# Column sums of the second half's last four squares on TensorE, and input chunks ahead of the last additions to x, in both feed-forward parts

## The chip, the cores and the metric

The kernel runs on one core of one Trainium2 chip. A core has TensorE (PE, matrix products), VectorE (DVE), ScalarE (ACT), GpSimd (POOL), and SyncE (SP), whose queue issues the transfers here. Each takes its instructions in program order and waits on semaphores. The metric is the device time of one execution in microseconds (us); lower is better. The kernel before takes 2377.08 us, the median of three runs (2376.66 to 2378.32).

## The reference

A backbone block of two layers over 1024 tokens of 1024 features, in float32. Layer 0 mixes tokens by latent attention, layer 1 by a short gated convolution; each is followed by a feed-forward part. What matters here is how each part normalises x and adds its result back:

```python
def rmsnorm(x, w):
    xf = x.astype(jnp.float32)
    y = xf * lax.rsqrt(jnp.mean(xf * xf, axis=-1, keepdims=True) + NORM_EPS)
    return (y * w.astype(jnp.float32)).astype(x.dtype)

def modulate(h, shift, scale):
    return h * (1 + scale) + shift
...
        x = x + g1 * y
        x = x + g2 * swiglu(modulate(rmsnorm(x, norm_ffn[i]), sh2, sc2),
                            ffn_w_gate[i], ffn_w_up[i], ffn_w_down[i])
```

## The kernel before

The program is written by hand for each engine, so its order on an engine is the order of the text. x is kept transposed: eight tiles of 128 features (m or k = 0 to 7), each with two halves of 512 tokens, A and B. Every product is made of three matmuls of 128x512 on a high and a low part of each operand (`mm3`, L607 to L609), named `_hi` and `_lo`.

An addition to x is `to_x(d, m, gate)` on DVE (L2071): bank m of the product d times the gate, plus x. A half's root mean square is a "job": ACT squares the eight x tiles (`squares_of`, L1393), POOL adds them one after another into one tile `acc` (`squares_sum`, L2766), PE sums that tile over its partitions against a column of ones (`job_sum`, L853: four products of 128x1, one for each 128 tokens), ACT takes the root (`job_sqrt`, L1400), DVE the reciprocal on a diagonal (`job_diag`), PE spreads it over all partitions (`job_bcast`, L871), and ACT copies that to `rstd` (`job_out`, L1405). Then the input chunks h of that half are made: for each k DVE scales x by `rstd` (`h_scaled`, L2285), ACT adds the shift and rounds to `h_hi` (L1628), and DVE makes `h_lo` (L2292). In `h_chunks`, DVE issues the scaling of chunk k+1 before the low part of k, since there are two buffers `tmp`.

A feed-forward part (`ffn_wino`; the first is f0, the second f1) begins with one block of four units in the plain form: unit 0 and 1 work on half A, unit 2 and 3 on half B (`inner`), each 8 chunks of 6 matmuls, into PSUM banks 0 and 1 or 2 and 3. After it come ten blocks in a Strassen-like form (`wino_block`), whose operands on the input's side (named T1 to T4) are sums of parts of h of both halves. The half-A statistic is ready ahead of unit 0. That of half B (jobs `J_MIX+1` and `J_MIX+5`, called job B here) is made in unit 0 and 1: its squares run between the A chunks, its column sum stands after chunk 5 of unit 0 and its broadcast after chunk 0 of unit 1. From the broadcast ACT and DVE then make the eight B chunks (`h_full_of`, `h_full_chunks`), multiply unit 1 (`silu_of`, `ffn_inner`), form T3, T1 and T2, and ACT rounds T2 (`b_top`) before it takes the SiLU of unit 3. The second product of the first Strassen-like block (GATE, "A12") writes to the bank that unit 3 used, so PE waits there for the SiLU of unit 3 (`bank_read`).

Ahead of each part stand the last additions of the half B of x: tiles 0 to 3 are added first, tiles 4 to 7 then take turns with the A chunks 0 to 3.

The buffers `raw` and `rq` share memory: `rq` (weights of the Strassen-like blocks) is loaded by SP once both `raw` tiles have been used.

## Time and profile before

| | |
|---|---|
| median of three runs | 2377.08 us (2376.66 to 2378.32) |
| profiled execution, its time | 2377.69 us |
| span of its trace | 2375.9 us |
| PE busy | 2334.4 us (98%) |
| DVE busy | 1690.1 us (71%) |
| ACT busy | 806.6 us (34%) |
| POOL busy | 151.2 us (6%) |
| mean granted TensorE clock | 0.992 of full speed |

Times in the rows below are microseconds from the start of the span. In a timeline row the first number is the start, the second the duration (of all instructions of a merged row), then the engine, line and operation; in brackets stands how long the engine had been idle and who released it. A matmul's duration overlaps that of the next, so the pace of PE is read from the distance of the starts. A float32 column product is recorded as two entries (x8 is four products). Unit 0 of f0 begins at 655.88 us, that of f1 at 1682.11 us.

### The profile page before, as it was taken

To read this page: it belongs to the slowest core of one execution; us is meant where nothing else is said; L and a number is where in the kernel's file an instruction comes from. 1 tells how busy PE (TensorE), PEld (TensorE's weight loads), DVE (VectorE), ACT (ScalarE), POOL (GpSimd) and SP (SyncE) were. 2 spreads that over 40 slices of the span, in tenths; PEclk is the share of its full clock that TensorE was granted. 3 is DMA by queue.
4 is the path that set the end of the run, shared out by engine and by line. 5 is a ranking of instruction groups with operands and counts; after the bars stand their busy time and mean duration, and the time that the engine had idled before them with its cause. 6 is when DMAs were issued, how large, how long until landed. Compare 5 with 4: busy or idle time off the path is not lost.

```text
span 2375.9 us, 29068 instructions
## 1 busy us (share of the span) xinstructions
PE 2334.4 (98%) x10989; PEld 1928.3 (81%) x10989; DVE 1690.1 (71%) x2495; ACT 806.6 (34%) x1279; POOL 151.2 (6%) x109
## 2 busy tenths in 40 slices
PE   7989999999999999999999999999999999999998
PEld 4878888887878888888888788888788888888887
DVE  4667777786589788888887763364897777777766
ACT  6345545454343222222222511111522222222224
POOL 0111111200210000000001200000200000000002
PEclk9999999999999999999999999999999999999998
DMA  7101111122201333333322020120101111111111
GB/s 290 38 25 43 42 42 51 42 80 107 80 36 62 107 107 107 107 107 107 107 98 89 18 71 27 45 72 27 45 28 53 54 54 54 54 52 51 52 50 71
DMA packets 48055, 163.33 MB, mean 69 GB/s; under 512 B 5185, under 2 KB 6593, under 8 KB 47809
## 3 DMA queue, kind: packets, MB, share of 16 engines
q1 hardware_dynamic: 47936, 161.72, 19.8%
q8 instruction: 78, 1.28, 0.2%
q14 instruction: 41, 0.33, 0.0%
HBM read 157.51 MB, written 4.19 MB: 68 GB/s over the span
## 4 chain that ended last, share of the span: by engine, by line
PE 94%; DVE 3%; ACT 1%; DMA 1%; POOL 0%; issue 0%; SPq 0%; ACTq 0%; DVEq 0%; POOLq 0%
PE ps L607 26%; PE ps L609 26%; PE ps L608 26%; PE ps L1062 3%; PE ps L996 2%; PE ps L1000 2%; PE ps L998 2%; PE ps L997 2%; PE ps L1001 1%; PE ps L1041 1%; PE ps L1043 1%; PE ps L1042 1%; DVE h_lo L2292 1%; DMA ada_ring<-ada_pe 1%; PE ps L1084 1%; PE ps L853 1%
## 5 line engine op out<-in xcount | busy, mean ns | idle before, releaser
L2071 DVE SCALAR_TENSOR_TENSOR x<-ps,mods,x 128x512 f32<-128x512 f32 x448 | 328.9, 748 | 151.4 <-PE ps L609 131.9
L607 PE MATMUL ps<-g_hi,w_hi 128*128 128x512 f32 x832 | 324.9, 390 | 0.8 <-DVE x L2071 0.6
L608 PE MATMUL ps<-g_lo,w_hi 128*128 128x512 f32 x832 | 323.8, 389 | 0.0
L609 PE MATMUL ps<-g_hi,w_lo 128*128 128x512 f32 x832 | 323.7, 389 | 0.0
L607 PE MATMUL ps<-h_hi,op_hi 128*128 128x512 f32 x640 | 249.2, 389 | 0.0
L609 PE MATMUL ps<-h_hi,op_lo 128*128 128x512 f32 x640 | 249.0, 389 | 0.0
L1657 ACT CAST op_hi<-rq 128x512 fp32r<-128x512 f32 x240 | 147.3, 623 | 235.6 <-PE ps L609 231.4
L1668 ACT ACTIVATE g_full<-g_full 128x512 f32<-128x512 f32 x80 | 50.8, 635 | 495.3 <-DVE g_full L2412 495.2
L607 PE MATMUL ps<-h_hi,w_hi 128*128 128x512 f32 x512 | 200.9, 392 | 7.5 <-DVE h_lo L2292 7.5
L609 PE MATMUL ps<-h_hi,w_lo 128*128 128x512 f32 x512 | 199.3, 389 | 0.0
L608 PE MATMUL ps<-h_lo,w_hi 128*128 128x512 f32 x512 | 199.3, 389 | 0.0
L608 PE MATMUL ps<-h_lo,op_hi 128*128 128x512 f32 x480 | 186.7, 389 | 0.0
L608 PE MATMUL ps<-w_lo,op_hi 128*128 128x512 f32 x480 | 186.7, 389 | 0.0
L607 PEld LDWEIGHTS ps<-g_hi,w_hi 128*128 128x128 f32 x832 | 156.2, 188 | 35.4 <-DVE x L2071 2.5
L609 PEld LDWEIGHTS ps<-g_hi,w_lo 128*128 128x128 f32 x832 | 156.2, 188 | 32.6
L608 PEld LDWEIGHTS ps<-g_lo,w_hi 128*128 128x128 f32 x832 | 156.2, 188 | 32.1
L1925 DVE TENSOR_TENSOR op_lo<-rq,op_hi 128x512 fp32r<-128x512 f32 x240 | 163.0, 687 | 1.1
L1925 DVE TENSOR_TENSOR pt_lo<-ps,pt_hi 128x512 fp32r<-128x512 f32 x160 | 110.1, 688 | 72.1 <-ACT pt_hi L1481 71.6
L609 PEld LDWEIGHTS ps<-h_hi,op_lo 128*128 128x128 f32 x640 | 120.1, 188 | 25.0
L607 PEld LDWEIGHTS ps<-h_hi,op_hi 128*128 128x128 f32 x640 | 120.2, 188 | 24.9
L1481 ACT CAST pt_hi<-ps 128x512 fp32r<-128x512 f32 x160 | 93.9, 587 | 131.3 <-PE ps L1062 131.3
L607 PE MATMUL ps<-w_hi,op_hi 128*128 128x512 f32 x320 | 124.5, 389 | 0.0
(345 smaller groups left out, 4569.7 us busy)
## 6 DMA issues: line engine op xcount, KB each, us to landing
rq<-stream SPq DMA_DIRECT2D x80, 512.0 KB, 3.5
mod_raw_f<-ada_rows SPq DMA_DIRECT2D x48, 512.0 KB, 3.6
raw<-stream SPq DMA_DIRECT2D x46, 512.0 KB, 3.6
w_lo_f<-stream SPq DMA_DIRECT2D x46, 512.0 KB, 4.4
mod_raw<-ada_rows SPq DMA_DIRECT2D x32, 512.0 KB, 3.5
ada_ring<-ada_pe SPq DMA_DIRECT2D x16, 512.0 KB, 10.9
x<-x_t SPq DMA_DIRECT2D x8, 512.0 KB, 7.3
out_t<-x SPq DMA_DIRECT2D x16, 256.0 KB, 2.1
```

The lines of the kernel that those rows point to most:

```text
L607: nc.tensor.matmul(out, w[0][wi], a[0][ai], start=start, stop=False)
L608: nc.tensor.matmul(out, w[0][wi], a[1][ai], start=False, stop=False)
L609: return nc.tensor.matmul(out, w[1][wi], a[0][ai], start=False, stop=stop)
L996: nc.tensor.matmul(dst, qa[par][0][:, q], ckv_hi[:, k0:k1], start=True, stop=False)
L997: nc.tensor.matmul(dst, qa[par][1][:, q], ckv_hi[:, k0:k1], start=False, stop=False)
L998: nc.tensor.matmul(dst, qa[par][0][:, q], ckv_lo[:, k0:k1], start=False, stop=False)
L1062: last = nc.tensor.transpose(ps[:, bank, j * P:(j + 1) * P], pbuf[:, 4 * (gb % 2) + j, k * P:(k + 1) * P], ident[:])
L1481: copy(pt_hi[:, (10 * gb + k) % 4, :], ps[:, bank, :]).then_inc(ra, 1)
L1657: copy(op_hi[:, at % 4, :], operand_a(s, mat, name)).then_inc(op_h, 1)
L1668: nc.scalar.activation(gate, gate, ACT.Silu).then_inc(corner_act, 1)
L1925: return nc.vector.tensor_tensor(dst, full, hi.bitcast(F32), ALU.subtract)
L2071: nc.vector.scalar_tensor_tensor(out=x[:, m, HALF[half]], in0=ps[:, out_bank(d, m), :], scalar=mods[:, gate + m:gate + m + 1], in1=x[:, m, ...
```

## The change

In both feed-forward parts:

- ACT squares tiles 0 to 3 of half B ahead of all A chunks, and POOL adds only these (three additions instead of seven).
- DVE makes all eight A chunks, and only then adds tiles 4 to 7 to x.
- ACT squares those four tiles into a buffer of their own, `sq_tail`, in memory that `rq` uses later. `job_sum` then sums five tiles (`acc` and the four of `sq_tail`) on PE: 20 column products instead of 4. SP's first `rq` loads now wait for this sum (`st_sum`) instead of for the product before.
- PE makes the sum after chunk 2 of unit 1 instead of chunk 5 of unit 0, and the broadcast after chunk 5 instead of chunk 0 of unit 1.
- ACT takes the SiLU of unit 0 before the root instead of after it, and rounds the second `down` tile behind the root. On DVE the products of unit 0 stand ahead of the diagonal.

```diff
--- before.py
+++ after.py
@@ -472,6 +472,7 @@
     mod_raw_f = sb("mod_raw_f", [D], F32, G1)
     sq_a = [sb(f"sq_a{k}", [HT], F32, X0 + 8192 + 2048 * k) for k in range(2)]
     acc_a = sb("acc_a", [HT], F32, N0)
+    sq_tail = sb("sq_tail", [4, HT], F32, X0)
     bsb = [sb(f"bsb{f}", [HT], F32, X0 + 2048 * f) for f in range(2)]
     zb = [sb(f"zb{f}", [T + 2], F32, X0 + 4096 + 4128 * f) for f in range(2)]
     op_hi, op_lo = sb("op_hi", [4, HT], F32R, N0), sb("op_lo", [4, HT], F32R, N0 + 8192)
@@ -559,6 +560,8 @@
     sq_end, fin_a, fin_p = sem("sq_end"), sem("fin_a"), sem("fin_p")
 
     sq_last = [tmp[0], tmp[1], ab[0], ab[1]]
+    tail_set = sem("tail_set")
+    TAIL_JOBS = (J_MIX + 1, J_MIX + 5)
 
     HALF = (slice(0, HT), slice(HT, T))
     ALL = slice(None)
@@ -797,7 +800,7 @@
                 modf_in(n)
 
         stream_in(12, 14)
-        sp.wait_ge(dn, 8 * D_F0)
+        sp.wait_ge(st_sum, J_MIX + 2)
         sp.wait_ge(t_lo, 14)
         quads_first(0)
         for s in range(WINO):
@@ -810,6 +813,7 @@
                     .then_inc(in_cv[n], 16)
         sp.wait_ge(op_l, product_n(WINO - 1, GATE, "S4") + 1)
         stream_in(14, len(TILES))
+        sp.wait_ge(st_sum, J_MIX + 6)
         sp.wait_ge(t_lo, len(TILES))
         quads_first(WINO)
         for s in range(WINO, 2 * WINO):
@@ -833,10 +837,13 @@
 
             bank = job_banks(j)[0]
             parts = (acc_of(j), sq[0]) if job_n(j) == QL else (acc_of(j),)
+            if j in TAIL_JOBS:
+                parts = (acc_of(j), *(sq_tail[:, n, :] for n in range(4)))
+                pe.wait_ge(tail_set, 4 * (TAIL_JOBS.index(j) + 1))
             if j <= J_XB:
                 pe.wait_ge(sq_row, j + 1)
             elif job_n(j) == D:
-                C.add("sqa", KD - 1)
+                C.add("sqa", 3 if j in TAIL_JOBS else KD - 1)
                 pe.wait_ge(sqa, C.at("sqa"))
             elif job_n(j) == QL:
                 C.add("q_sq", 2)
@@ -1302,8 +1309,8 @@
 
         def ffn_wino(phase, turn, job_b, job_a):
 
-            inner(phase, 0, 0, turn, (job_b, 5), None)
-            inner(phase, 0, 1, turn, None, (job_b, 0))
+            inner(phase, 0, 0, turn, None, None)
+            inner(phase, 0, 1, turn, (job_b, 2), (job_b, 5))
             inner(phase, 0, 2, turn, None, None)
             inner(phase, 0, 3, turn, None, None)
             for s in range(WINO):
@@ -1621,6 +1628,12 @@
             act.wait_ge(xe, 8 * d + m + 1)
             squares(j, m, x[:, m, HALF[j % 2]], HT)
 
+        def squares_tail(j, d):
+
+            for n in range(4):
+                act.wait_ge(xe, 8 * d + n + 5)
+                nc.scalar.activation(sq_tail[:, n, :], x[:, n + 4, HALF[j % 2]], ACT.Square).then_inc(tail_set, 1)
+
         def h_top_of(turn, half, k):
 
             shift, _ = AFTER[turn]
@@ -1753,10 +1766,11 @@
         def ffn_wino(phase, turn, d_before, jobs_b, jobs_a):
 
             s0 = 0 if phase == "f0" else WINO
-            for f in range(2):
-                top(phase, 0, "down", f, (dn, 8 * d_before + 8))
+            squares_tail(jobs_b, d_before)
+            top(phase, 0, "down", 0, (dn, 8 * d_before + 8))
+            silu_of(phase, 0, 0)
             job_sqrt(jobs_b)
-            silu_of(phase, 0, 0)
+            top(phase, 0, "down", 1, (dn, 8 * d_before + 8))
             job_out(jobs_b)
             for k in range(KD):
                 h_full_of(turn, k)
@@ -1868,12 +1882,10 @@
                 gate_out(blk, "b", B, 1)
                 job_sqrt(jobs_a)
                 job_out(jobs_a)
-                for m in range(3):
+                for m in range(4):
                     squares_of(jobs_a + 1, d + 1, m)
                 for k in range(KD):
                     h_top_of(turn + 1, A, k)
-                    if k < 5:
-                        squares_of(jobs_a + 1, d + 1, k + 3)
 
         for n in range(4, 6):
             top("out", 0, "wo", n)
@@ -1897,12 +1909,10 @@
         job_sqrt(J_MIX)
         job_out(J_MIX)
         act.wait_ge(sv_set, 1)
-        for m in range(3):
+        for m in range(4):
             squares_of(J_MIX + 1, D_OUT + 3, m)
         for k in range(KD):
             h_top_of(0, A, k)
-            if k < 5:
-                squares_of(J_MIX + 1, D_OUT + 3, k + 3)
         ffn_wino("f0", 0, D_OUT + 3, J_MIX + 1, J_MIX + 2)
         conv_start(1, J_MIX + 3)
         conv(1, J_MIX + 3, J_MIX + 4)
@@ -2555,10 +2565,10 @@
         def ffn_wino(phase, turn, gate, job_b, job_a):
 
             s0 = 0 if phase == "f0" else WINO
-            for f in range(2):
-                low(phase, 0, "down", f)
+            ffn_inner(phase, 0, 0)
+            low(phase, 0, "down", 0)
             job_diag(job_b)
-            ffn_inner(phase, 0, 0)
+            low(phase, 0, "down", 1)
             h_full_chunks(turn)
             ffn_inner(phase, 0, 1)
             operand_low(s0, 0)
@@ -2707,10 +2717,9 @@
                 job_diag(job_a)
                 to_x(d_b, 2, gate)
                 to_x(d_b, 3, gate)
-                for k in range(4):
-                    h_chunks(turn + 1, A, k, k + 1)
-                    to_x(d_b, k + 4, gate)
-                h_chunks(turn + 1, A, 4, KD)
+                h_chunks(turn + 1, A, 0, KD)
+                for m in range(4, KD):
+                    to_x(d_b, m, gate)
 
         rest = slice(N_PE_MOD + N_ATT_MOD - 8, N_PE_MOD + N_ATT_MOD)
         dve.wait_ge(mod_out, passes + 1)
@@ -2744,10 +2753,9 @@
         to_x(D_OUT + 3, 2, GATES[0])
         to_x(D_OUT + 3, 3, GATES[0])
         dve.wait_ge(sv_set, 1)
-        for k in range(4):
-            h_chunks(0, A, k, k + 1)
-            to_x(D_OUT + 3, k + 4, GATES[0])
-        h_chunks(0, A, 4, KD)
+        h_chunks(0, A, 0, KD)
+        for m in range(4, KD):
+            to_x(D_OUT + 3, m, GATES[0])
         ffn_wino("f0", 0, GATES[1], J_MIX + 1, J_MIX + 2)
         conv_start(1, GATES[1])
         conv(1, GATES[2], J_MIX + 3, J_MIX + 4)
@@ -2806,12 +2814,10 @@
 
         def squares_sum(j):
 
-            for m in range(1, KD):
+            for m in range(1, 4 if j in TAIL_JOBS else KD):
                 add_squares(j, m, HT)
 
-        squares_sum(J_MIX)
-        squares_sum(J_MIX + 1)
-        for j in range(J_MIX + 2, J_MIX + 7):
+        for j in range(J_MIX, J_MIX + 7):
             squares_sum(j)
         for m in range(1, KD // 2):
             add_squares(J_MIX + 7, m, HT)
```

In the rows of the program's order below, PE stands in unit 0 of f0 before, at the column sum of job B (`acc_104` is its accumulated tile):

```order
L608 MATMUL ps<-h_lo,w_hi 128x512
L609 MATMUL ps<-h_hi,w_lo 128x512
L853 MATMUL ps<-ones,acc_104 128x1 x4
L607 MATMUL ps<-h_hi,w_hi 128x512
L608 MATMUL ps<-h_lo,w_hi 128x512
L609 MATMUL ps<-h_hi,w_lo 128x512
```

And in unit 1 of f0 now, between chunk 2 and chunk 3 (each `x4` row is the four `sq_tail` tiles):

```order
L612 MATMUL ps<-h_hi,w_lo 128x512
L860 MATMUL ps<-ones,acc_104 128x1
L860 MATMUL ps<-ones,sq_tail 128x1 x4
L860 MATMUL ps<-ones,acc_104 128x1
L860 MATMUL ps<-ones,sq_tail 128x1 x4
L860 MATMUL ps<-ones,acc_104 128x1
L860 MATMUL ps<-ones,sq_tail 128x1 x4
L860 MATMUL ps<-ones,acc_104 128x1
L860 MATMUL ps<-ones,sq_tail 128x1 x4
L610 MATMUL ps<-h_hi,w_hi 128x512
```

The sum has moved from unit 0 to unit 1 and has grown from 4 column products to 20.

DVE at the start of f0 before, from the first A chunk (`tmp` is the scaled x, L2071 an addition to x):

```order
L2292 SCALAR_TENSOR_TENSOR h_lo<-tmp_107,mods,h_hi 128x512
L2071 SCALAR_TENSOR_TENSOR x<-ps,mods,x 128x512
L2285 SCALAR_TENSOR_TENSOR tmp_107<-x,svec,rstd_105 128x512
L2292 SCALAR_TENSOR_TENSOR h_lo<-tmp_108,mods,h_hi 128x512
L2071 SCALAR_TENSOR_TENSOR x<-ps,mods,x 128x512
L2285 SCALAR_TENSOR_TENSOR tmp_108<-x,svec,rstd_105 128x512
L2292 SCALAR_TENSOR_TENSOR h_lo<-tmp_107,mods,h_hi 128x512
L2071 SCALAR_TENSOR_TENSOR x<-ps,mods,x 128x512
```

DVE there now, from the last A chunks to job B's reciprocal:

```order
L2295 SCALAR_TENSOR_TENSOR tmp_108<-x,svec,rstd_105 128x512
L2302 SCALAR_TENSOR_TENSOR h_lo<-tmp_107,mods,h_hi 128x512
L2302 SCALAR_TENSOR_TENSOR h_lo<-tmp_108,mods,h_hi 128x512
L2081 SCALAR_TENSOR_TENSOR x<-ps,mods,x 128x512 x4
L2322 TENSOR_TENSOR ab_153<-ab_153,ps 128x512
L2325 CAST g_hi<-ab_153 128x512
L1935 TENSOR_TENSOR g_lo<-ab_153,g_hi 128x512
L1935 TENSOR_TENSOR w_lo<-raw_109,w_hi 128x1024
L1941 RECIPROCAL rr<-sd 128x4
L1944 TENSOR_TENSOR diag<-ident,rr 128x512
L1935 TENSOR_TENSOR w_lo<-raw_110,w_hi 128x1024
```

The additions stood between the chunks and now stand behind the last one; the multiplication of unit 0 (`ab`) and one low part of a `down` tile have moved ahead of the reciprocal.

ACT around job B's root in f0 before (`sd` is the root, `ab` the SiLU):

```order
L1628 ACTIVATE h_hi<-tmp_108,mods 128x512 [waits s_h_mul]
L1413 CAST w_hi<-raw_109 128x1024 [waits s_dn,s_in_raw0]
L1413 CAST w_hi<-raw_110 128x1024 [waits s_dn,s_in_raw1]
L1400 ACTIVATE sd<-ps,eps_c 128x4 [waits s_st_dg,s_st_sum]
L1636 ACT_TABLE_LOAD
L1636 ACTIVATE ab_153<-ps 128x512 [waits s_pj]
L1405 COPY rstd_106<-ps 128x512 [waits s_st_bc]
L1642 ACTIVATE w_hi_f<-tmp_107,mods 128x512 [waits s_h_mul]
```

ACT there now:

```order
L1635 ACTIVATE sq_tail<-x 128x512 [waits s_xe] x4
L1420 CAST w_hi<-raw_109 128x1024 [waits s_dn,s_in_raw0]
L1649 ACT_TABLE_LOAD
L1649 ACTIVATE ab_153<-ps 128x512 [waits s_pj]
L1407 ACT_TABLE_LOAD [waits s_st_dg]
L1407 ACTIVATE sd<-ps,eps_c 128x4 [waits s_st_sum]
L1420 CAST w_hi<-raw_110 128x1024 [waits s_dn,s_in_raw1]
L1412 COPY rstd_106<-ps 128x512 [waits s_st_bc]
L1655 ACTIVATE w_hi_f<-tmp_107,mods 128x512 [waits s_h_mul]
```

And ACT now at the SiLU of unit 1, behind the last B chunk:

```order
L1655 ACTIVATE w_lo_f<-tmp_108,mods 128x512 [waits s_h_mul]
L1658 CAST h_hi<-w_lo_f 128x512 [waits s_b_set]
L1649 ACT_TABLE_LOAD
L1649 ACTIVATE ab_154<-ps 128x512 [waits s_pj]
L1670 CAST op_hi<-rq 128x512 [waits s_in_q0,s_n_lo]
L1670 CAST op_hi<-rq 128x512 [waits s_in_q0]
```

The order SiLU, root, SiLU takes three loads of ACT's function table where one stood: one ahead of the first SiLU, one ahead of the root and one ahead of the SiLU of unit 1, which had none of its own.

## Rows read from the trace of the kernel before

**Rows 1.** The page: busy time by engine, and the chain that ended last

```profile
PE 2334.4 (98%) x10989; PEld 1928.3 (81%) x10989; DVE 1690.1 (71%) x2495; ACT 806.6 (34%) x1279; POOL 151.2 (6%) x109
...
PE 94%; DVE 3%; ACT 1%; DMA 1%; POOL 0%; issue 0%; SPq 0%; ACTq 0%; DVEq 0%; POOLq 0%
```

**Rows 2.** Waits of PE, whole run: who waited, for whom, us, times, longest

```profile
PE ps L607 <- DVE h_lo L2292: 7.5, 6, 1.7
```

**Rows 3.** Timeline, PE, f0: start of unit 0, and the broadcast of job B

```profile
655.88 0.39 PE L607 MATMUL ps<-h_hi,w_hi 128*128 128x512 f32 x1
...
671.89 1.05 PE L871 MATMUL ps<-diag,ones 128*128 128x128 f32 x8
```

**Rows 4.** Timeline, PE, f1: unit 0, the sum and the broadcast of job B

```profile
1682.11 0.43 PE L607 MATMUL ps<-h_hi,w_hi 128*128 128x512 f32 x1
...
1697.03 0.95 PE L853 MATMUL ps<-ones,acc 128*128 128x1 f32 x8
1697.83 0.47 PE L607 MATMUL ps<-h_hi,w_hi 128*128 128x512 f32 x1
...
1702.04 1.05 PE L871 MATMUL ps<-diag,ones 128*128 128x128 f32 x8
```

**Rows 5.** Timeline, DVE, f1: an A chunk while POOL adds, and two without it

```profile
1692.29 1.75 DVE L2292 SCALAR_TENSOR_TENSOR h_lo<-tmp,mods,h_hi 128x512 fp32r<-128x512 f32 x1
1694.07 0.75 DVE L2285 SCALAR_TENSOR_TENSOR tmp<-x,svec,rstd 128x512 f32<-128x512 f32 x1
...
1695.52 0.75 DVE L2285 SCALAR_TENSOR_TENSOR tmp<-x,svec,rstd 128x512 f32<-128x512 f32 x1
```

**Rows 6.** Timeline, ACT, f1: first h_hi, the table load, SiLU of units 0 and 1

```profile
1682.01 0.71 ACT L1628 ACTIVATE h_hi<-tmp,mods 128x512 fp32r<-128x512 f32 x1
...
1699.10 1.28 ACT L1636 ACT_TABLE_LOAD   x1
1700.39 0.60 ACT L1636 ACTIVATE ab<-ps 128x512 f32<-128x512 f32 x1
...
1716.01 0.60 ACT L1636 ACTIVATE ab<-ps 128x512 f32<-128x512 f32 x1
```

**Rows 7.** Timeline, PE, a sum of eight column products (16 entries), and what follows

```profile
72.99 0.28 PE L853 MATMUL ps<-ones,acc 128*128 128x1 f32 x2
...
74.69 0.47 PE L607 MATMUL ps<-x0a_hi,sw_hi 128*128 128x512 f32 x1
```

**Rows 8.** Timeline, DVE, ACT, PE, f1: unit 1 multiplied, to the second product (1736.97)

```profile
1716.74 0.68 DVE L2312 TENSOR_TENSOR ab<-ab,ps 128x512 f32<-128x512 f32 x1
...
1734.15 1.92 ACT L1662 CAST w_hi<-w_lo_f 128x2048 fp32r<-128x2048 f32 x1 [9.64 <-DVE w_lo_f L2377]
1735.97 0.59 ACT L1636 ACTIVATE ab<-ps 128x512 f32<-128x512 f32 x1
...
1736.29 0.39 PE L607 MATMUL ps<-h_hi,op_hi 128*128 128x512 f32 x1
...
1736.97 0.39 PE L607 MATMUL ps<-h_hi,op_hi 128*128 128x512 f32 x1
```

**Rows 9.** The same in f0: SiLU of unit 3, and the second product

```profile
705.83 0.59 ACT L1636 ACTIVATE ab<-ps 128x512 f32<-128x512 f32 x1
...
706.82 0.39 PE L607 MATMUL ps<-h_hi,op_hi 128*128 128x512 f32 x1
```

**Rows 10.** Timeline, PE: two restarts after a wait, and the end of the first slow stretch

```profile
29.65 0.76 PE L607 MATMUL ps<-x0a_hi,sw_hi 128*128 128x512 f32 x1 [2.58 <-DVE sw_lo L1964]
...
34.05 0.47 PE L608 MATMUL ps<-x0a_lo,sw_hi 128*128 128x512 f32 x1
...
123.13 0.58 PE L996 MATMUL ps<-ckv_hi,qa_hi 128*128 128x256 f32 x1 [3.25 <-ACT pbuf L1518]
```

**Rows 11.** Windows, closing column sum (from 2356.3): PE, PEld, DVE, ACT, POOL busy, then PEclk

```profile
2357.00:2358.00 1.00, 1.00 (x12) 1.00 (x11) 1.00 (x3) 0.63 (x1) 0.00 (x0) 1.00 0.62 240
...
2359.00:2360.00 1.00, 1.00 (x7) 1.00 (x6) 1.00 (x3) 0.98 (x2) 0.00 (x0) 0.50 0.39 150
```


## The prediction

> **What bounds the kernel now.** I read the page first: PE is busy for 98% of the span, and 94% of the chain that ended last is PE's [rows 1]. So only time in which PE stands still, or work put on PE, can move the end. The list of PE's waits comes next. Its largest entry that belongs to the feed-forward parts is the wait for `h_lo`: 7.5 us in 6 waits [rows 2], all in unit 0 of f0 and f1. The timeline gives the true size of what can be won. Three wide matmuls take 1736.97 - 1736.29 = 0.68 us [rows 8], so one is 0.227 us, a chunk of six 1.36 us and a unit of eight chunks 10.88 us. In f1, unit 0 starts at 1682.11 and its chunk 6 at 1697.83 [rows 4]; less six chunks (8.16) and the sum (0.80) that is 6.8 us of standing still. In f0 the broadcast starts at 671.89, 16.01 us after unit 0 [rows 3]; nine chunks (12.24) and the sum take 13.0 of it, so some 2.9 us are lost, 9.7 us together. The last thing I read is what follows the broadcast of job B, since the change makes it later: the rows from unit 1 on to the second product of the first Strassen-like block [rows 8, 9].
>
> **Part 1: A chunks ahead of the additions.** An A chunk takes DVE 1695.52 - 1694.07 = 1.45 us where nothing interferes, and the low part alone 1.75 us while POOL adds [rows 5]. PE uses one each 1.36 us. With the four additions behind the chunks (four times some 0.67 us) and four POOL additions gone, DVE keeps up with PE nearly as soon as it has begun. It begins later: ACT now squares tile 3 ahead of the first `h_hi`. That square waits for POOL and stood between the first and the second `h_hi`; the first now takes the place of the second, 1682.01 to 1682.72 [rows 6], so the first chunk is ready at about 1683.8, and with POOL still adding for two chunks the last at about 1694.5. In f1 PE waits 1.7 us at the start and some 1.3 us later: unit 0 ends at 1694.5 + 1.36 = 1695.9. In f0 the lead is greater: behind half A's broadcast PE still has three output tiles of 12 matmuls, in f1 three of 6, so 18 x 0.227 = 4.1 us more. What comes 1.7 us late there comes 2.4 early here, and the last chunk, 12.4 us behind PE's start there, comes 8.3 behind it here, where PE wants it at 9.5. Unit 0 starts at 655.88 [rows 3] and ends at 655.9 + 10.9 = 666.8 with no wait. The wait on `h_lo` shrinks from 9.7 to some 3 us. The additions themselves are covered: the banks that they free are next used by the part's first `down` product, more than 30 us later, and with the four squares behind them they end about 3.5 us after the last chunk, near 668 and 1698, ahead of the sum at 670.8 and 1700.0.
>
> **Part 2: the sum on PE.** Eight column products took 74.69 - 72.99 = 1.70 us [rows 7] and four take 0.80 [rows 4], so one more costs 0.22 us, and twenty cost 0.80 + 16 x 0.225 = 4.4 us. PE pays 3.6 us more in each part, 7.2 us in all, with nothing to hide it. The nearest row below is the same sum if its products ran in the pace of the four (0.20, 4.0 us); above it, at half clock, 8.8 us.
>
> **Part 3: the broadcast comes later.** f0: unit 0 ends at 666.8, three chunks to 670.8, the sum to 675.2, three chunks to 679.3: the broadcast starts 7.4 us later than the 671.89 of now [rows 3]. f1: 1695.9, 1700.0, 1704.4, 1708.5: 6.4 us later than 1702.04 [rows 4]. Root and diagonal (about 1.4 us) fit into the three chunks. Behind the broadcast the same work as now follows on ACT and DVE: copy, eight B chunks, product of unit 1, T3, T1, T2, and almost none of it waits. In f1 the product of unit 1 starts at 1716.74, ACT waits 9.64 us for T2, rounds it at 1734.15, and the SiLU of unit 3 ends at 1735.97 + 0.59 = 1736.56; the product that needs it starts at 1736.97 [rows 8]. In f0 it is 706.42 against 706.82 [rows 9]. This chain has 0.4 us of slack. What is late in it is late on PE.
>
> **Part 4: table loads.** A load takes 1.28 us, 1699.10 to 1700.39 [rows 6]. The one ahead of the root ends before the sum does. The one ahead of the SiLU of unit 1 does not hide: ACT is the engine that works up to 1716.01, and DVE starts the product of unit 1 (1716.74 [rows 8]) 0.13 us after this SiLU ends (1716.61 [rows 6]), held by its own last low part. With 1.28 more on ACT it starts 1.2 us later.
> The Trainium skill (ScalarE: Activation LUTs, What ACT_TABLE_LOAD costs) puts a switch at 1.28 us plus a drain of 1.38, 2.66 in all. The rows show the load following the root at once and the SiLU following the load at once. By the page's figure the chain would be 1.4 us later in each part and the estimate of the whole 2.8 us higher.
>
> **The sum without the clock.** The second product starts later by 7.4 + 1.2 - 0.4 = 8.2 us in f0 and by 6.4 + 1.2 - 0.4 = 7.2 us in f1. These are against the trace's own times, so what PE wins in unit 0 is in them already: PE loses it again, as it then stands still. Between unit 1's product and the SiLU of unit 3 the chain takes 1736.56 - 1716.74 + the multiply's 0.7, about 19.1 us; PE has a unit and a product, 13.6 us, so it waits some 5.5 us for the second product in each part. From there on DVE is as late as PE, and nothing in the later blocks gives it back. Sum: +15.4 us. SP's `rq` loads start 7 us later, at about 678, and are needed at 695: hidden.
>
> **The clock.** Waits of 2.58 and 3.25 us are followed by PE at 1.2 instead of 2.4 GHz: from 29.65 to 34.05 ten matmuls take 4.40 us instead of 2.27 [rows 10], a loss of 2.1 us. How long PE stays slow may differ; as an estimate, a stretch two thirds or four thirds as long would cost 1.4 or 2.8. A wait of 5.5 us will do the same as these two: +2.1 in each part, 4.2. And column products alone let the clock fall too: in the kernel's closing sum it is at 1.00 in the second microsecond and at 0.50 in the fourth [rows 11]. A sum of 4.4 us would be slowed over its last 1.8 us: +1.8 in each part, 3.6, from 0 (the 1.70 us sum of rows 7 was not slowed) to 2.8 each if it stays slow into the matmuls.
>
> **The forecast.** 2377.7 (the profiled execution; the median of the runs is 0.6 less) + 15.4 + 4.2 + 3.6 = 2400.9; against the median 2400.3. I say 2400.3 us, 1.0% slower.
>
> **Rivals.**
> 1. *The chain is late, but the clock does not fall, or only after the waits.* For it: the sum of rows 7 kept its clock. Time: 2377.1 + 15.4 = 2392.5 to 2396.7.
> 2. *The chain has cover that I don't see.* T2 might not be what holds the SiLU of unit 3, or the first waits in unit 2 might be shorter. Then what remains is 9.7 us won, less 3 of wait left and 7.2 of sum: 0.5 us slower, 2377.6, and if unit 0 has no wait left at all 2.5 us faster, 2374.6. Against it: the 9.64 us wait of rows 8 ends exactly with T2, and the two parts agree to 0.01 us. Cover of a part of the delay is possible: each microsecond of it saves one in each part.
> 3. *Faster by over 0.2%: column products that hide behind wide matmuls.* If their weight loads overlapped the neighbours the sum would cost PE under 1 us, the broadcast would start only 3 to 4 us later, and if in addition the chain had 4 us of slack, PE would keep the 6.7 us won: 2370.4. It decides from a sum under 2 us on. Against it: rows 7 show each product paid in full.
> 4. *More than the forecast.* Both clock losses at their upper end (2.8 each, 11.2) give 2377.1 + 15.4 + 11.2 = 2403.7; a slowed sum also makes the broadcast wait, and the drain of the table load adds up to 2.8.
> 5. *The change does not do what it says*, unit 0 goes on waiting because 1.45 is more than 1.36 us: 0.1 us per chunk, inside the forecast.
>
> **How the numbers follow.** Forecast with both clock losses, 2398 to 2403: 0.45. Rival 1: 0.33. Rival 4: 0.10. Rival 2: 0.09. Rival 3: 0.03. The range of 8 in 10 takes the forecast, rival 1 with 1.5 us a part for errors of my ready times, and rival 4: 2389 to 2406. 0.2% (4.8 us) is what a measurement of this kernel can tell from no change: faster 0.03, same 0.09, slower 0.88.
>
> **What would show it.** In the changed trace: (a) PE's waits on the A chunks in unit 0 are about 0 in f0 and 3 us in f1. (b) The sum lasts 4.4 us, or 6 with the clock at 0.50 in its end. (c) The broadcast starts 12.6 us behind the end of unit 0, near 679.3 and 1708.5. (d) PE waits 1 to 2 us for B chunks in unit 2, and about 5.5 us ahead of the second product of the first Strassen-like block, on ACT's SiLU, behind the rounding of T2. (e) The granted clock is 0.50 behind that wait. (f) A table load stands ahead of the SiLU of unit 1. The forecast is wrong if (d) is missing: then the time is within 0.2%. It is too high if (d) is there without (e).

## The result, and the profile after

The kernel after takes 2398.52 us, the median of five runs (2397.43 to 2398.67), beside 2378.32 (2376.66 to 2378.75) of five runs of the kernel before: a ratio of 1.0087, 95% interval 1.0076 to 1.0099. The profiled execution took 2398.67 us, its span is 2397.4, its mean clock 0.991.

The page after, busy time by engine and the chain, in the form of [rows 1]:

```profile
PE 2348.2 (98%) x11053; PEld 1937.6 (81%) x11053; DVE 1683.8 (70%) x2495; ACT 810.5 (34%) x1283; POOL 138.9 (6%) x101
...
PE 93%; DVE 4%; ACT 1%; issue 1%; DMA 1%; POOL 1%; SPq 0%; ACTq 0%; POOLq 0%; DVEq 0%
```

POOL and DVE got less work, PE more, and the shares don't show that anything is wrong. PE's waits do (who waited, for whom, us, times, longest), against the 7.5 us of [rows 2]:

```profile
PE ps L610 <- ACT ab L1649: 10.1, 2, 5.1
...
PE ps L610 <- DVE h_lo L2302: 2.0, 2, 1.4
PE ps L610 <- DVE h_lo L1935: 1.9, 2, 1.0
```

The wait on the A chunks (L2302) has shrunk as meant. In its place stands one of 5 us in each part on a SiLU, and a small one on the B chunks (L1935). PE's timeline in f0, from the sum to the broadcast and at the second product of the first Strassen-like block (compare [rows 3] and [rows 9]):

```profile
670.91 0.28 PE L860 MATMUL ps<-ones,acc 128*128 128x1 f32 x2
...
675.29 0.49 PE L610 MATMUL ps<-h_hi,w_hi 128*128 128x512 f32 x1
...
676.81 0.63 PE L612 MATMUL ps<-h_hi,w_lo 128*128 128x512 f32 x1
677.23 0.63 PE L610 MATMUL ps<-h_hi,w_hi 128*128 128x512 f32 x1
...
681.11 1.05 PE L878 MATMUL ps<-diag,ones 128*128 128x128 f32 x8
...
716.95 0.60 PE L610 MATMUL ps<-h_hi,op_hi 128*128 128x512 f32 x1 [5.05 <-ACT ab L1649]
717.35 0.63 PE L611 MATMUL ps<-h_lo,op_hi 128*128 128x512 f32 x1
717.78 0.63 PE L612 MATMUL ps<-h_hi,op_lo 128*128 128x512 f32 x1
```

The sum lasts 675.29 - 670.91 = 4.38 us, at full pace. Behind it four wide matmuls still run at full pace or near it, then eight stand 0.43 us apart instead of 0.227; behind the 5.05 us wait there are nine more. The windows of these microseconds (PE, PEld, DVE, ACT, POOL busy, then PEclk) show the granted clock at 1.00 in the sum and at 0.50, which is 1.2 of 2.4 GHz, behind it:

```profile
674.00:675.00 1.00, 1.00 (x11) 1.00 (x11) 0.00 (x0) 0.00 (x0) 0.00 (x0) 1.00 0.00 0
676.00:677.00 1.00, 1.00 (x5) 0.75 (x4) 0.97 (x2) 0.67 (x1) 0.00 (x0) 0.62 0.02 8
678.00:679.00 1.00, 1.00 (x4) 0.72 (x3) 0.00 (x0) 0.00 (x0) 0.00 (x0) 0.50 0.04 12
```

What holds the SiLU is seen on ACT in f0, against [rows 8]:

```profile
695.16 1.28 ACT L1649 ACT_TABLE_LOAD   x1
696.46 0.60 ACT L1649 ACTIVATE ab<-ps 128x512 f32<-128x512 f32 x1
...
714.50 1.90 ACT L1675 CAST w_hi<-w_lo_f 128x2048 fp32r<-128x2048 f32 x1 [14.89 <-DVE w_lo_f L2387]
716.31 0.59 ACT L1649 ACTIVATE ab<-ps 128x512 f32<-128x512 f32 x1
```

ACT stands 14.89 us for T2, rounds it, and only then takes the SiLU of unit 3.

**The account by stages.** Each entry is the distance between two starts in a run's timeline (the last one to the end of the span), so a column adds up to the span. "Broadcast" is job B's unless A is named; "second product" is that of the first Strassen-like block.

| us | before | after | difference |
|---|---|---|---|
| start to unit 0 of f0 | 655.88 | 655.95 | +0.07 |
| f0: unit 0 to broadcast | 16.01 | 25.16 | +9.15 |
| f0: broadcast to second product | 34.93 | 35.84 | +0.91 |
| to job A's broadcast ahead of f1 | 970.28 | 971.99 | +1.71 |
| f1: job A's to job B's broadcast | 24.94 | 33.20 | +8.26 |
| f1: broadcast to second product | 34.93 | 35.84 | +0.91 |
| to the closing column sum | 619.32 | 621.08 | +1.76 |
| closing sum to last broadcast | 7.63 | 6.30 | -1.33 |
| to the end | 12.0 | 12.0 | 0.0 |

### The profile page after: what moved, and what is told of

It is laid out like the page before. It is cut to its first block, busy times and chain, and to the rows that moved or that the text cites. A ratio compares the mean times of both kernels' runs of the same rounds, so it can differ in the third digit from the quotient of the medians.

```text
span 2397.4 us, 29177 instructions
## 1 busy us (share of the span) xinstructions
PE 2348.2 (98%) x11053; PEld 1937.6 (81%) x11053; DVE 1683.8 (70%) x2495; ACT 810.5 (34%) x1283; POOL 138.9 (6%) x101
## 4 chain that ended last, share of the span: by engine, by line
PE 93%; DVE 4%; ACT 1%; issue 1%; DMA 1%; POOL 1%; SPq 0%; ACTq 0%; POOLq 0%; DVEq 0%
PE ps L610 25%; PE ps L611 25%; PE ps L612 25%; PE ps L1069 3%; PE ps L1003 2%; PE ps L1005 1%; PE ps L1007 1%; PE ps L1004 1%; PE ps L1008 1%; PE ps L1048 1%; PE ps L1050 1%; PE ps L1049 1%; PE ps L860 1%; DMA ada_ring<-ada_pe 1%; PE ps L1091 1%
## 5 line engine op out<-in xcount | busy, mean ns | idle before, releaser
L1935 DVE TENSOR_TENSOR op_lo<-rq,op_hi 128x512 fp32r<-128x512 f32 x240 | 162.7, 686 | 1.0
L1935 DVE TENSOR_TENSOR pt_lo<-ps,pt_hi 128x512 fp32r<-128x512 f32 x160 | 110.0, 688 | 72.1 <-ACT pt_hi L1488 71.6
```

What stands on the lines that cost most here:

```text
L1935: return nc.vector.tensor_tensor(dst, full, hi.bitcast(F32), ALU.subtract)
```

## The experiments

The kernel before ran beside each group of runs: 2376.83, 2377.80, 2377.10 and 2376.98 us in the four groups. "Of before" and "of after" below say which kernel was edited.

**1. Delay alone.** Of before: only the broadcast is moved, from chunk 0 to chunk 3 of unit 1.

```diff
-            inner(phase, 0, 1, turn, None, (job_b, 0))
+            inner(phase, 0, 1, turn, None, (job_b, 3))
```

> The kernel before with one edit: job B's broadcast stands after chunk 3 of unit 1 instead of after chunk 0, in both parts. PE's work is the same. Theory C (the chain behind the broadcast sets when the second product can start, with 0.4 us of slack): the broadcast starts 4.1 us later, PE waits about 3.7 us for the SiLU of unit 3 in each part, +7.4 us, and the clock falls behind that wait for another 1 to 2 us each: 2385.5 to 2389. Rival W (only PE's own work counts, the chain has cover): no change, 2378.

2387.64 us (2385.70 to 2388.75), ratio 1.0044 (1.0030 to 1.0058), inside theory C's range. PE in f0:

```profile
676.04 1.05 PE L871 MATMUL ps<-diag,ones 128*128 128x128 f32 x8
...
710.59 0.79 PE L607 MATMUL ps<-h_hi,op_hi 128*128 128x512 f32 x1 [3.53 <-ACT ab L1636]
```

The broadcast is three chunks later (20.03 us behind unit 0's start instead of 16.01), no work was added, and the same wait on the SiLU of unit 3 appears. Broadcast to second product is 34.55 us (34.53 in f1) instead of 34.93: of 4.02 us of delay the chain covers 0.38, the rest reaches PE. The clock fell behind both waits. Rival W falls.

**2. Less delay.** Of after: the broadcast two chunks earlier.

```diff
-            inner(phase, 0, 1, turn, (job_b, 2), (job_b, 5))
+            inner(phase, 0, 1, turn, (job_b, 2), (job_b, 3))
```

> The changed kernel with its broadcast after chunk 3 of unit 1 instead of chunk 5. PE's work is the same. Theory C: the broadcast is 2.7 us earlier, up to 4 where these two chunks ran at the lower clock, and the second product as much: -5 to -8 us, 2390 to 2393; PE still waits some 4 us for it. Rival W: no change, 2398.5.

2397.36 us (2392.59 to 2397.43), ratio 1.0078 (1.0061 to 1.0095): the median misses C's range (one run of four, 2392.59, lies in it) and is 1 us under W. PE in f0, behind the wait:

```profile
714.62 0.79 PE L610 MATMUL ps<-h_hi,op_hi 128*128 128x512 f32 x1 [4.82 <-ACT ab L1649]
715.22 0.63 PE L611 MATMUL ps<-h_lo,op_hi 128*128 128x512 f32 x1
...
720.34 0.60 PE L611 MATMUL ps<-g_lo,w_hi 128*128 128x512 f32 x1
```

By stages, the second product comes 2.78 us earlier behind unit 0's start than in after (21.51 + 36.71 = 58.22 against 61.00), as C says. It could be 3.65 (25.16 - 21.51), but the broadcast stood in the slow stretch and took 0.87 us longer. The clock took more back: 13 matmuls at 0.43 us behind each wait instead of 9 (the stages behind the two second products are 1.31 and 1.19 us longer), and in f1 the end of the sum was itself slow, so that the second product there came only 1.14 us earlier. So the chain is confirmed in f0 by its stage, not by the time of the whole, since the clock took most of the gain back. What makes the slow stretch longer in one program than in another, these runs don't say.

**3. The sum on POOL.** Of after: POOL adds all eight squares, PE makes four column products.

```diff
-                parts = (acc_of(j), *(sq_tail[:, n, :] for n in range(4)))
...
-                act.wait_ge(xe, 8 * d + n + 5)
-                nc.scalar.activation(sq_tail[:, n, :], x[:, n + 4, HALF[j % 2]], ACT.Square).then_inc(tail_set, 1)
+                squares_of(j, d, n + 4)
...
```

> The changed kernel, but the four late squares are added by POOL again, so that PE's sum has 4 column products instead of 20; order, place of sum and broadcast are those of the changed kernel. If the sum costs PE 3.6 us and the granted clock falls because of its length, the sum takes 0.8 us, the clock stays at full behind it, the broadcast starts 5.4 us earlier in each part: -11 us, 2387.5. If the clock falls for another reason: -7.2, 2391. Either way more than 5 us above the kernel before, since the order alone makes the broadcast late.

2391.40 us (2391.26 to 2392.11), ratio 1.0059 (1.0042 to 1.0076). That is the time of the second forecast (the clock falls for another reason), but the stages show the first one's mechanism. Unit 0 to broadcast is 19.97 us instead of 25.16 in f0, and 4.27 less in f1, where PE waited 0.66 us for POOL; no slow matmul follows the sum. In f0 the gain is 3.6 for the column products and 1.6 for the clock. Behind the waits of 5.04 and 5.07 us 11 matmuls were slow instead of 9, which took 0.8 us back in each part, and the stretch ahead of f0 took 1.4 us more than in after, which the edit doesn't touch.

**4. The SiLU of unit 3 first.** Of after: ACT takes it ahead of the rounding of T2.

```diff
-            act.wait_ge(pj, unit_pj(phase, 0, 2))
-            b_top(phase, "T2")
             silu_of(phase, 0, 3)
+            b_top(phase, "T2")
```

> The changed kernel with one edit on ACT: the SiLU of unit 3 stands ahead of the rounding of T2 instead of behind it. Theory C names that order as what holds the second product: its wait of 5.1 us goes; PE waits next for the low part of unit 3 ahead of the first down product, 2 us at most, and the clock does not fall: -3 us in each part and up to -5 with the clock, 2388.5 to 2392.5. Rival W, or a chain that is held elsewhere (PE waits the same time one product later): 2398.

2390.46 us (2390.14 to 2392.94), ratio 1.0059 (1.0042 to 1.0075), inside theory C's range. The second product comes 5.2 us earlier in each part (30.65 us behind the broadcast instead of 35.84), and no slow stretch follows. What holds the second product is this one position in ACT's order. PE now waits at the first `down` product instead:

```profile
715.23 0.47 PE L610 MATMUL ps<-g_hi,w_hi 128*128 128x512 f32 x1 [1.69 <-issue]
```

**5. The sum in two pieces.** Of after: ten column products behind chunk 1 of unit 1, ten behind chunk 2.

```diff
-                if sum_at is not None and k == sum_at[1]:
+                if sum_at is not None and half == A and sum_at[1] == 2 and k in (1, 2):
+                    job_sum(sum_at[0], (0, 1) if k == 1 else (2, 3))
+                elif sum_at is not None and k == sum_at[1]:
...
```

> The kernel after, with one edit: PE makes the column sum of job B in two pieces, ten column products behind chunk 1 of unit 1 and ten behind chunk 2 (after: all twenty behind chunk 2). Work and end of the sum are the same. Theory C (a long row of column products lets the clock fall, and that costs about 1.8 us in each part): each piece takes 2.2 us, the wide matmuls behind both stand at 0.227 us, the broadcast starts about 1.8 us earlier, and since it stands in the chain that sets the second product of the first Strassen-like block, the time falls by 2 x 1.8 = 3.6 us: 2393 to 2396. Rival W (the clock falls for another reason at that time, the waits on POOL and ACT or the stretch as a whole): slow matmuls at 0.43 us stay behind one of the two pieces and the time stays at 2397 to 2399.

2405.93 us (2404.10 to 2407.36), ratio 1.0121 (1.0105 to 1.0136): slower than both forecasts. PE in f0, both pieces:

```profile
669.51 1.03 PE L863 MATMUL ps<-ones,sq_tail 128*128 128x1 f32 x8
...
672.86 0.63 PE L612 MATMUL ps<-h_hi,w_lo 128*128 128x512 f32 x1
...
673.57 1.84 PE L863 MATMUL ps<-ones,sq_tail 128*128 128x1 f32 x8
...
678.41 0.63 PE L612 MATMUL ps<-h_hi,w_lo 128*128 128x512 f32 x1
```

The first piece takes 2.15 us, but the sixth matmul behind it is already slow, the second piece runs at half clock (673.29 to 677.41, 4.12 us), and the matmuls stay slow up to 682.7. The broadcast comes 3.24 us later than in after. So it is the column products that bring the clock down, and six wide matmuls between two pieces don't prevent it; my picture that only an unbroken row of them does is wrong. (Experiments 3 and 7 show the same from both sides: with four column products nothing behind the sum is slow, with twenty in the kernel before it is.)

**6. The root first.** Of after: root ahead of the SiLU of unit 0 again, which spares two table loads a part.

```diff
             top(phase, 0, "down", 0, (dn, 8 * d_before + 8))
-            silu_of(phase, 0, 0)
             job_sqrt(jobs_b)
+            silu_of(phase, 0, 0)
...
-            ffn_inner(phase, 0, 0)
             low(phase, 0, "down", 0)
             job_diag(job_b)
+            ffn_inner(phase, 0, 0)
```

> The kernel after, with one edit: ACT takes the root ahead of the SiLU of unit 0 again, and DVE makes the first low part and the diagonal ahead of the product of unit 0, as the kernel before did. The SiLU of unit 1 then follows a SiLU with no table load of its own; two loads of 1.28 us fewer in each part. Theory T (a load ahead of the SiLU of unit 1 stands in the chain): DVE multiplies unit 1 1.2 us earlier behind the broadcast and the second product of the first Strassen-like block starts 1.2 us earlier in each part: 2395 to 2397. Rival D (DVE, not ACT, holds that multiplication: its own last low part ends no earlier): the load is gone, the second product does not move, 2398 to 2399.

2398.32 us (2397.64 to 2398.82), ratio 1.0089 (1.0074 to 1.0104). By the time rival D; by the stages theory T: broadcast to second product is 34.54 us in both parts instead of 35.84, so the load ahead of the SiLU of unit 1 did stand in the chain, with 1.30 us. The clock took it back (0.86 us behind f0's wait, 1.60 in f1 before the broadcast, where the sum's end ran slow).
The Trainium skill (ScalarE: Activation LUTs, What ACT_TABLE_LOAD costs) has 1.28 us plus a drain of 1.38 for a switch; here the chain got shorter by 1.30 when the load went, so no drain shows.

**7. Only the longer sum.** Of before: order and places as they are, but PE sums five tiles with 20 column products.

```diff
+            if j in TAIL_JOBS and m >= 4:
+                nc.scalar.activation(sq_tail[:, m - 4, :], x[:, m, HALF[j % 2]], ACT.Square).then_inc(tail_set, 1)
+                return
...
-            for m in range(1, KD):
+            for m in range(1, 4 if j in TAIL_JOBS else KD):
...
```

> The kernel before, with the sum alone changed: the last four squares of job B go to a buffer of their own and PE sums five tiles with 20 column products, after chunk 5 of unit 0 as before; order on ACT and DVE, and the places of sum and broadcast, are those of before. Theory C: PE pays 3.6 us a part for the longer sum, less what POOL's additions cost DVE in unit 0, and the slower clock behind the sum: 2380 to 2386 (ratio 1.0015 to 1.004); the broadcast comes some 3 to 5 us later than before, and of that the chain behind it hands on all but 0.4 us. Rival: the column products themselves are what costs the change its time, 2390 and more. Rival: they cost nothing, since PE waits in unit 0 anyway: 2377.

2382.66 us (2381.89 to 2384.40), ratio 1.0023 (1.0014 to 1.0032), inside theory C's range. PE in f0, the start of the sum, the first wide matmul behind it, and the first of the eight slow ones:

```profile
663.57 0.28 PE L860 MATMUL ps<-ones,acc 128*128 128x1 f32 x2
...
667.95 0.49 PE L610 MATMUL ps<-h_hi,w_hi 128*128 128x512 f32 x1
...
669.04 0.63 PE L611 MATMUL ps<-h_lo,w_hi 128*128 128x512 f32 x1
669.47 0.63 PE L612 MATMUL ps<-h_hi,w_lo 128*128 128x512 f32 x1
```

The broadcast comes 2.40 us later in f0 and 4.01 in f1, broadcast to second product stays at 34.9: here the broadcast is late only because PE is, and the chain and PE stay together. PE's waits on the A chunks fell from the 7.5 us of [rows 2] to 2.6, where POOL adds less beside DVE, and that pays for a part of the longer sum and of the slow stretch behind it (8 and 11 matmuls). So in its old place the longer sum costs 4.9 us net of what it saves, a quarter of the change's 20 us; the rest comes with the later places.

**8. Four repairs at once.** Of after: edits 2, 3 and 4, and DVE forms T1 behind the last additions to x of the first Strassen-like block instead of ahead of unit 2's product.

```diff
             b_part(phase, "T3")
-            b_part(phase, "T1")
             ffn_inner(phase, 0, 2)
...
             for m in range(4, KD):
                 to_x(d_was, m, gate)
+            if at_first(s):
+                b_part(phase, "T1")
...
```

> The kernel after, with four edits together: POOL adds the last four squares (no sum on PE of more than four column products), the broadcast stands behind chunk 3 of unit 1, ACT takes the SiLU of unit 3 ahead of the rounding of T2, and DVE forms T1 later, behind the last additions to x of the first Strassen-like block. Theory C (what the change loses is the longer sum, the fallen clock and a chain behind the broadcast that holds the second product): with the chain cut short on both sides PE keeps what it wins in unit 0. Against the kernel before: 6.7 us won in unit 0, no more sum, 1 to 2 us lost to waits in unit 2: 2368 to 2372, a ratio of 0.997. Rival D (DVE is busy nearly all the time from the broadcast to the second block, so whatever PE wins it loses as a wait on another product of DVE): a new wait of 5 to 8 us a part on DVE or ACT inside the first blocks, 2376 to 2385.

2379.74 us (2377.88 to 2382.84), ratio 1.0011 (1.0002 to 1.0020): rival D's range, not theory C's. The waits on the SiLU, the long sum and nearly all slow matmuls are gone, and still it is not faster than before. DVE and PE in f0 show the new wait:

```profile
671.79 0.69 DVE L2317 TENSOR_TENSOR ab<-ab,ps 128x512 f32<-128x512 f32 x1 [5.11 <-ACT ab L1645]
...
674.92 0.69 DVE L1939 TENSOR_TENSOR diag<-ident,rr 128x512 f32<-128x512 f32 x1
```

```profile
675.67 1.67 PE L875 MATMUL ps<-diag,ones 128*128 128x128 f32 x8 [2.08 <-DVE diag L1939]
```

The diagonal stands on DVE behind unit 0's product, which waits for a SiLU. A second wait, of 1.39 us a part, stands later in the first block; neither is as long as the 5 to 8 us that rival D named, and the first is a matter of order.

**9. With the root first too.** Edit 6 on top.

> The kernel of the last run (after, with POOL adding the last squares, the broadcast behind chunk 3 of unit 1, the SiLU of unit 3 ahead of T2's rounding, T1 formed late), with a fifth edit: ACT takes the root ahead of the SiLU of unit 0, and DVE the diagonal ahead of unit 0's product. There PE waited 2.08 and 2.16 us for the diagonal, which stood on DVE behind that product and a low part of 1.22 us, and behind two table loads on ACT. Theory O (only these two waits and the T1 wait of 1.4 us a part stand between it and PE's gain): the broadcast starts 2.1 us earlier in each part, the slow stretch behind it (1 us) goes, the wait ahead of T1's product stays at 1.4 or falls to 0.2: 2372 to 2375.5, a ratio near 0.998. Rival D (DVE is the bound): the time won turns up as a longer wait for T1 or for another operand in the first blocks, and the time stays within 1 us of 2379.7.

2377.30 us (2375.65 to 2378.44), ratio 1.0001 (0.9992 to 1.0010): between the two forecasts, 1.8 us above theory O's range and 1.4 under the lower end of D's. No wait stands between the sum and the broadcast, and no slow matmul in either part. Against before, with three chunks more (4.08 us) ahead of the broadcast: unit 0 to broadcast 16.01 + 4.08 - 17.25 = 2.84 us won in f0, 24.94 + 4.08 - 26.20 = 2.82 in f1. Behind it 32.04 instead of 34.93 - 4.08 = 30.85 us to the second product, since PE now takes the B chunks in unit 2 as they come, and 1.67 more after that, 2.86 lost. The 1.67 is mostly this wait of PE, with what DVE does just then:

```profile
729.65 0.47 PE L610 MATMUL ps<-w_hi,op_hi 128*128 128x512 f32 x1 [1.38 <-issue]
```

```profile
677.62 0.69 DVE L1930 TENSOR_TENSOR h_lo<-w_hi_f,h_hi 128x512 fp32r<-128x512 f32 x1 [0.78 <-ACT h_hi L1654]
...
728.86 0.68 DVE L1930 TENSOR_TENSOR op_lo<-op_full,op_hi 128x512 fp32r<-128x512 f32 x1
729.47 0.68 DVE L2417 TENSOR_TENSOR part_ug<-part_ug,ps 128x512 f32<-128x512 f32 x1
```

"issue" names no engine, but the matmul starts 0.11 us after `op_lo`, its operand, is written. From 677.62 to the end of that write DVE is busy for 49.5 us of 51.9: it rests for 2.4 us, of which 1.6 in three waits (the 1.6 of the expectation of experiment 11 are these three alone).

**10. T1 2.6 us earlier.** As 9, with T1 formed ahead of the last four additions.

> The same with one edit more: DVE forms T1 ahead of the last four additions to x of the first Strassen-like block instead of behind them, 2.6 us earlier. Theory O: the wait of 1.4 us a part ahead of T1's product is gone, nothing else waits for those additions: 2370 to 2373. Rival D: PE now waits for the banks that those additions free, 1 to 4 us a part, and the time is that of the run before or above it.

2377.78 us (2376.12 to 2378.73), ratio 1.0003 (0.9994 to 1.0012). The wait is unchanged, 1.37 us at 731.33. The time is as rival D says, but both mechanisms fall: PE waits neither for T1 (formed 2.6 us earlier, nothing moved) nor for the banks that the additions free. It waits for the operand behind both, and their sum is the same in either order.

**11. Less work on DVE.** As 9, T1's second subtraction (2.28 us) left out, so this kernel doesn't compute the whole of the block.

```diff
-                own(nc.vector.tensor_tensor(b12, b12, b11[0].bitcast(F32), ALU.subtract))
-                nc.vector.tensor_tensor(b12, b12, b11[1].bitcast(F32), ALU.subtract).then_inc(b_sum, 1)
+                nc.vector.tensor_tensor(b12, b12, b11[0].bitcast(F32), ALU.subtract).then_inc(b_sum, 1)
```

> The kernel with the five edits (root first, T1 formed late), and of T1's two subtractions on DVE, 2.28 us each, the second is left out (the low part of h of half A isn't subtracted, once in each feed-forward part). In the two runs before, PE waited 1.38 us in each part ahead of its seventh product of the first Strassen-like block, on no engine that the profile names; DVE wrote that product's low operand just then (728.86 to 729.54), and had worked from 677.62 on with 1.6 us of idle time. Theory D (DVE's work between the broadcast and this operand is the bound): with 2.2 us less of it the wait goes to 0 in both parts, and the time falls by 2.8 us to 2374 to 2375. Rival I (the wait is PE's own sequencer, as the profile's word says): it stays at 1.38 us and the time at 2377.3.

2373.83 us (2372.43 to 2375.18), ratio 0.9984 (0.9975 to 0.9993). That is just under theory D's 2374 to 2375, and well under rival I's 2377.3. The wait is gone in both parts, and the stages behind the second products are those of before, 970.24 and 619.32 us. DVE's work is what held it.

**12. The same work in a better order.** As 9, T1's second subtraction behind the operand that PE waited for (and on ACT the rounding of T1 behind the first operand of the products with T1).

```diff
             operand_low(s, 6)
+            if at_first(s):
+                b_part(phase, "T1b")
...
```

> The same with five edits and nothing left out, but T1's second subtraction stands on DVE behind the low part of the seventh product's operand, and ACT rounds T1 behind the first operand of the products with T1. Theory D: the wait of 1.38 us ahead of the seventh product goes; T1's low part ends at about the time of before while PE wants it 1.4 us earlier, so a wait of 0.4 to 1 us a part stands ahead of the ninth product, the first with T1: 2375.3 to 2376.6. Rival I: the wait ahead of the seventh product stays, and 2377.3 or more is measured.

2374.50 us (2372.90 to 2375.66), ratio 0.9989 (0.9980 to 0.9998), 0.8 us under the range of theory D; rival I falls. What is left of the wait stands where expected, at the first product with T1, on T1's low part:

```profile
734.90 0.47 PE L610 MATMUL ps<-w_hi,op_hi 128*128 128x512 f32 x1 [0.45 <-DVE w_hi L1931]
```

This is the one complete kernel of the study below the kernel before, by 0.1%; its interval just leaves 1 out. Of the 3.8 us between its span and that of before, the stages from unit 0 of f0 to the closing sum make 1.6; the closing sum took 6.32 us instead of 7.63 and the stretch ahead of f0 0.9 us less, which is no merit of the edits (last section).

## Why the prediction was right

- **Part 1** held. f0's unit 0 has no wait (670.91 - 655.95 = 14.96 us for eleven chunks, forecast 670.8 for the sum). In f1 the waits on A chunks are listed with 1.38 and 0.66 us. By the starts they cost the 3.0 us forecast: unit 0 starts 6.55 us behind job A's broadcast instead of 5.01, and from there to the sum PE takes 16.44 us where 14.96 is the time without a wait. (The `h_hi` at 1682.01 of [rows 6], called the first, is the second, as Part 1 uses it.)
- **Part 2**: 4.38 us against 4.4.
- **Part 3**: broadcast +9.15 and +8.26 us, against 7.4 + 1.8 and 6.4 + 1.8 with the clock. The slack of 0.4 us in the chain was measured by experiment 1 as 0.38 and 0.40.
- **Part 4**: the table load costs 1.30 us in the chain (experiment 6) against 1.2; load less slack gives +0.91 in both parts (35.84 - 34.93), against +0.8.
- **The waits**: 5.05 and 5.07 us ahead of the second product against 5.5, and 0.94 and 0.96 in unit 2 for B chunks where 1 to 2 were said, both on the engines named. Experiments 1 and 4 show the mechanism from both sides. The 19.1 us from which the 5.5 was worked out is 19.82 less the multiply's 0.68; the text of the prediction adds it, its number is right.
- **The clock in the sum** is the step whose size held and whose place didn't: the sum itself ran at full pace, and the eight matmuls behind it lost 1.7 us. The 1.8 forecast was the part of the sum beyond the point where the closing sum slows down, so that it came out is in part luck, and experiment 5 shows that the picture behind it was too simple.
- **The clock behind the waits** was oversized: nine slow matmuls and +1.71 and +1.76 us, not 2.1.
- **Not foreseen**: the closing sum took 1.33 us less. With the clock behind the waits (0.7 us less than said) and the time outside the span (1.27 us instead of 1.79), less 0.3 of small excesses, that makes the 2.2 us between the forecast for the profiled execution (2400.9) and its 2398.67.

What the prediction did not ask is how full the chain behind the broadcast is. It said that this chain takes back what PE wins in unit 0, as if its place alone mattered. Experiments 9, 11 and 12 show the bound behind that: from the broadcast to the first block's seventh product DVE is nearly full (49.5 us of 51.9 in experiment 9), so the 2.8 us a part that PE wins in unit 0 come back as waits until DVE's work is less or better ordered.

## What to carry to other kernels

A wait is worth removing only if the chain that starts behind it has slack: follow the engine that is next to be late, and count its idle time up to the next point where the two meet. When a step is moved later, price it by the chain that hangs on it, not by the step. One instruction in a queue (a rounding ahead of a SiLU) held PE for 5 us in each part here, and swapping the two is the cheap repair: experiment 4 is at a ratio of 1.0059 where the change is at 1.0087.

## What the runs showed of the hardware

- Column products of 128x1 took 0.22 us each and brought the clock down. Twenty in a row kept full pace in after, and eight wide matmuls behind them were slow (8 and 11 in experiment 7); in f1 of experiments 2, 4, 6 and 7 the last column products were slow too. Four in a row had no slow matmul behind them (experiment 3). With ten, six wide matmuls and ten more, the second ten ran at half clock (experiment 5).
- After a wait of 3.5 to 5 us, 6 to 13 matmuls stood 0.43 us apart, and after 2.08 and 2.16 us (experiment 8) five and none. The number isn't set by the wait: 3.53 us was followed by 6 in f0 and 11 in f1 of experiment 1, 5.05 by 9 in after, 5.04 by 11 in experiment 3.
- The kernel's closing sum, the same 20 column products in every run, took from 5.81 to 7.63 us up to the last broadcast. In after:

```profile
2379.06 0.95 PE L1375 MATMUL ps<-ones,acc 128*128 128x1 f32 x8
...
2385.36 3.78 PE L1381 MATMUL ps<-diag,ones 128*128 128x128 f32 x16 [1.29 <-DVE diag L1944]
```

Where in it the clock falls differs, so about 2 us of a difference between two profiled executions of this kernel can come from its end, whatever was changed. The stretch ahead of f0's unit 0 differs as much: it took from 654.34 to 657.32 us, and 654.34 and 656.03 in experiments 9 and 10, whose programs are the same up to there. Why wasn't looked into. So a gain of 1 or 2 us is read from the stages that an edit touches, or from many runs, and not from two spans.
